# Down products with high and low parts as one moving operand of 512 columns

## The chip, the core and the metric

The kernel runs on one core of one Trainium2 chip. The metric is the device time of one execution in microseconds (us); a lower number is better. The engines named are TensorE (PE, matmuls), ScalarE (ACT), VectorE (DVE), GpSimd (POOL) and SyncE (SP, which issues the loads of weights).

## The reference

A first block of two layers, then a second block of two layers, on 256 tokens of width 1024 in float32. Only the feed-forward parts matter here. Block 1 has two per layer, one ahead of its mixer and one behind it:

```python
def swiglu(x, w1, w2):
    gu = x @ w1
    g, u = gu[..., :D_FF], gu[..., D_FF:]
    return (jax.nn.silu(g) * u) @ w2

for l in range(DEPTH):                       # DEPTH = 2, D_FF = 2816
    x = x + 0.5 * swiglu(rms_norm(x, ffn1_norm[l]), ffn1_w1[l], ffn1_w2[l])
    x = x + hybrid_mixer(rms_norm(x, mix_norm[l]), ...)
    x = x + 0.5 * swiglu(rms_norm(x, ffn2_norm[l]), ffn2_w1[l], ffn2_w2[l])
return rms_norm(x, final_norm)
```

Block 2 has one feed-forward part per layer, with a short convolution over the tokens between its two products, and a norm behind the second. The change leaves its products as they are.

## The kernel before, in words

**Data.** Everything is kept transposed: a tile is 128 features (partitions) x 256 tokens (T). x has 8 such tiles (KT), the hidden layer of a feed-forward part 22 (FT). To keep float32 accuracy on the faster fp32r matmul, each operand is split into a high part (rounded to fp32r) and a low part (what is left). A product (`product`, L600 to L607) of one 128x128 weight block with one tile is three matmuls of 256 columns into the same 256 columns of a bank: high weights x high part (L605), high weights x low part (L606), low weights x high part (L607). A bank (`banks`) holds 512 columns, used as two halves of 256.

**Weights.** They come as a stream of units of up to 16 blocks, 1 MB; the down units have 11 blocks, 704 KB. SP loads a unit into one of two raw slots (`load_unit`, L568), as soon as the unit two before it has been split. ACT casts it to `w_hi` (`split_hi`, L578) and DVE subtracts to get `w_lo` (`split_lo`, L584). There are four split slots; the cast of a unit waits until TensorE is done with the unit four before it. TensorE waits for `w_lo` (`weights_ready`). Every engine runs its own program in a fixed order written out by hand; semaphores alone tie them together. So on ACT and DVE the splits stand in a fixed place between the other work.

**A feed-forward part** (`ffn_pe`, `ffn_act`, `ffn_dve`). Up: 22 units, each 8 blocks for the gate half and 8 for the other half, into the halves of banks 0 to 3 in turn. DVE scales a bank by the norm (L835), ACT applies SiLU (L799), DVE multiplies the halves to `hid` (L840), ACT casts to `hid_hi` (L802), DVE subtracts to `hid_lo` (L846). Down: 8 output tiles, each 2 units of 11 blocks, so 22 products into columns 0 to 255 of bank 2 or 3 in turn. When a tile is done, DVE adds half the bank to x (`residual`, L865) and frees the bank; ACT squares the new x for the next norm (L721) and makes the next input's high part `h_hi` (L690), DVE its low part `h_lo` (L695). GpSimd sums the squares (L732).

**Order around the down products.** ACT: cast of the tile's first unit, square and h_hi of the tile, cast of its second unit. DVE: w_lo of the first unit, the residual, w_lo of the second, h_lo. The splits run four units ahead, so the last ones belong to what comes next: the mixer's `pa` units behind the first feed-forward part of a layer, the next layer's up units (or block 2's first units) behind the second. Behind the first part TensorE goes on with the mixer's products tile by tile (L640 to L642), and comes to the norm's matmuls after four tiles (48 matmuls). Behind the second part of layer 0 it starts the next up units (L617, L619), and these wait until banks 0 to 3 are all free.

**Loops.** TensorE's up loop is 2 units by `first_products` and then 5 rounds of 4 units; the down loop has 4 rounds of 2 tiles. ACT and DVE have 4 rounds of 4 units in the up part with the rest written out.

`Groups` and `Work` do the bookkeeping of which bank a group of products takes and who frees it; `wait_banks_free` and `bank_free` read it.

Of the kernel before, what the change touches and what calls it, by code (L numbers as in the profile page):

```python
# [23 lines left out]
T = 256  # L24
# [95 lines left out]
class Groups:  # L120


    def __init__(self, steps, freer=FREER, fixed=FIXED_BANK):
        self.mark, self.bank, self.freer = {}, {}, {}
        marks = 0
        self.freed_until, main, last, self.before = {"a": 0, "v": 0}, 0, {}, {}
        for kind, i in steps:
            g = (kind, i)
            if kind in NOT_ON_PE:
                continue  # L130
            if kind == "K":
# [22 lines left out]
            self.before[g] = last.get(bank)  # L154
# [4 lines left out]
            last[bank] = g  # L159
        self.marks, self.last = marks, last  # L160
# [119 lines left out]
def build(nc, io):  # L280
    with ExitStack() as ctx:
# [8 lines left out]
        h_hi = sbuf("h_hi", [P, KT, T], F32R)  # L290
        h_lo = sbuf("h_lo", [P, KT, T], F32R)
# [110 lines left out]
        class Work:  # L402
# [15 lines left out]
            def bank_free(self, layer, group):  # L418

                before = self.g.before[group]  # L420
                wrapped = before is None
                before = before or self.g.last[self.g.bank[group]]
                who, n = self.g.freer[before]
                s = self.freed[who]
                return s(layer, n - s.per) if wrapped else s(layer, n)

            def wait_banks_free(self, pe, layer, groups, taken=()):
# [6 lines left out]
                for group in groups:  # L434
                    before = self.g.before[group]
                    wrapped = before is None
                    who, n = self.g.freer[before or self.g.last[self.g.bank[group]]]
                    latest[who] = max(latest.get(who, -10 ** 9), n - (self.freed[who].per if wrapped else 0))
# [169 lines left out]

        def first_products(pe, nm, work, l, m, groups, stat):
# [131 lines left out]
        def ffn_pe(pe, work, nm, l, w, at, n, m, hidden, raw_units):  # L741
# [11 lines left out]

            work.wait_banks_free(pe, l, [(up, j) for j in range(4)])
            weights_ready(pe, at + 1)
            if raw_units:
# [7 lines left out]
                with pe.Fori(0, 4) as it:  # L764
                    for u in range(4):
                        pe.wait_ge(*work.taken(l, (up, 0), it * 4 + u))
                        up_unit(4 + u, it * 4)
                for j in range(20, FT):
                    pe.wait_ge(*work.taken(l, (up, j - 4)))
                    up_unit(j, 0)  # L770
            else:
                first_products(pe, nm, work, l, m, [((up, j), at + j) for j in range(2)], lambda: norm_pe(pe, work, nm, l, n))
                with pe.Fori(0, 5) as it:
                    for u in range(4):
                        pe.wait_ge(*work.taken(l, (up, 0), it * 4 + (2 + u - 4)))
                        up_unit(2 + u, it * 4)
            with pe.Fori(0, KT // 2) as it:
                for g in range(2):
# [3 lines left out]
                    for half in range(2):  # L782
# [3 lines left out]
                        for b in range(HALF):  # L786
                            k = half * HALF + b
                            if k >= FT - 3:
                                pe.wait_ge(*hidden(l, w * FT + k + 1))
                            last = product(pe, banks[2 + g][:, 0:T], s, b, hid_hi[:, k], hid_lo[:, k],  # L790
                                           k == 0, k == FT - 1)
                        last.then_inc(work.done_sem.sem, 1)

        def ffn_act(act, l, w, at, then, split):
# [8 lines left out]

            with act.Fori(0, 4) as it:
                for u in range(4):
                    gated(u, it * 4, u % 2, lambda: split_hi(act, at + u + FFN_AHEAD, it * 4, it * 2))
            split.next = at + 16 + FFN_AHEAD
            for j in range(16, FT):
# [20 lines left out]
        def ffn_dve(dve, l, w, at, n, then, split):  # L829
            up, down, work = f"up{w}", f"down{w}", work1  # L830

            def gated(j, more, parity, split_next, before=True):
                bank = banks[j % 4]
                dve.wait_ge(*work.done(l, (up, 0), more + j))
                dve.tensor_tensor(halves(scaled[:, parity]), halves(bank[:, :]), by_r(2),  # L835
# [14 lines left out]
            for j in range(2):  # L850
                gated(j, 0, j % 2, lambda: split.until(at + j + FFN_AHEAD), j > 0)
            with dve.Fori(0, 4) as it:
                for u in range(2, 6):
                    gated(u, it * 4, u % 2, lambda: split_lo(dve, at + u + FFN_AHEAD, it * 4))
            split.next = at + 18 + FFN_AHEAD
            for j in range(18, FT):
# [1466 lines left out]
```

## Time and profile before

| | us |
|---|---|
| median of 3 runs | 2327.35 |
| lowest and highest | 2321.9, 2327.54 |
| the profiled execution's own time | 2319.62 |
| its span, first to last instruction | 2317.8 |
| TensorE busy | 2045.6 (88%) |
| VectorE busy | 1472.7 (64%) |
| ScalarE busy | 1168.3 (50%) |
| mean granted TensorE clock | 0.931 |

Times of rows are us from the start of the span. Matmuls are pipelined: the duration of one (280 ns) is its way through the array, and what it costs in a stream is the distance between two starts. "Idle before" is idle time of the engine ahead of an instruction, with what ended it. The chain of waits is followed back from the last instruction, at each step to what released it. PEclk is the granted clock, 1.00 being 2.4 GHz and 0.50 being 1.2 GHz.

### The profile page before, as it was taken

Reading aid. Unit: us, or ns where it says so; the run is one execution under the profiler, and the core shown is the slowest. Engines: PE = TensorE matmul, PEld = TensorE weight load, DVE = VectorE, ACT = ScalarE, POOL = GpSimd, SP = SyncE. Lnnn points to the kernel's source line nnn. Section 1 sums busy time; section 2 is a strip of 40 time slices with the busy share of each in tenths; the row PEclk is TensorE's granted clock in tenths of the full one; section 3 lists DMA queues with packets and bytes.
Section 4 is the critical chain, followed back from the end, with each engine's and each line's share of the span. In section 5 each row is a group of like instructions: output and inputs, shape, how many; then the busy total and the mean of one; then the engine's idle time right before and its main releaser. Section 6 shows DMA issues by size and latency. Waiting matters only on the chain.

```text
span 2317.8 us, 40039 instructions
## 1 busy us (share of the span) xinstructions
PE 2045.6 (88%) x15496; PEld 1951.3 (84%) x15496; DVE 1472.7 (64%) x2084; ACT 1168.3 (50%) x1804; POOL 149.5 (6%) x167
## 2 busy tenths in 40 slices
PE   6999877879999999878879998787899978887998
PEld 6999867879999999867879998665799976667998
DVE  5665698655655655698656655564598465626963
ACT  5445644444444445644444445554565445536753
POOL 0071000000000001000000001000300000003000
PEclk9999989989999999989989999887899988878999
DMA  5545323345545545323345454331254532202543
GB/s 206 182 167 184 128 100 109 118 165 173 178 163 191 184 162 184 128 100 110 123 161 180 170 170 156 109 109 37 73 197 157 190 125 98 103 19 106 210 147 118
DMA packets 53535, 329.83 MB, mean 142 GB/s; under 512 B 5936, under 2 KB 6704, under 8 KB 27952
## 3 DMA queue, kind: packets, MB, share of 16 engines
q1 hardware_dynamic: 53424, 328.34, 41.0%
q8 instruction: 71, 1.16, 0.2%
q14 instruction: 40, 0.33, 0.0%
HBM read 327.27 MB, written 1.05 MB: 142 GB/s over the span
## 4 chain that ended last, share of the span: by engine, by line
PE 49%; DVE 16%; ACT 12%; issue 10%; DVEq 7%; DMA 3%; POOLq 3%; POOL 1%; ACTq 0%; SPq 0%
PE bank L605 13%; PE bank L606 13%; PE bank L607 13%; DVE w_lo L584 7%; ACT w_hi L578 5%; DMA raw<-in_w 2%; DVEq L915 2%; DVE conv L1239 2%; DVEq L1233 2%; PE bank L617 1%; ACT probs L924 1%; PE bank L626 1%; PE bank L619 1%; PE bank L1522 1%; PE bank L1538 1%
## 5 line engine op out<-in xcount | busy, mean ns | idle before, releaser
L584 DVE TENSOR_TENSOR w_lo<-raw,w_hi 128x2048 fp32r<-128x2048 f32 (+3 forms) x358 | 719.2, 2010 | 433.1 <-ACT w_hi L578 430.6
L605 PE MATMUL bank<-h_hi,w_hi 128*128 128x256 f32 x2704 | 784.9, 290 | 17.7 <-DVE w_lo L584 16.4
L606 PE MATMUL bank<-h_lo,w_hi 128*128 128x256 f32 x2704 | 775.7, 287 | 0.0
L607 PE MATMUL bank<-h_hi,w_lo 128*128 128x256 f32 x2704 | 774.9, 287 | 0.0
L578 ACT ACTIVATE w_hi<-raw 128x2048 fp32r<-128x2048 f32 (+3 forms) x358 | 600.9, 1680 | 170.7 <-DMA raw<-in_w 118.3
L605 PEld LDWEIGHTS bank<-h_hi,w_hi 128*128 128x128 f32 x2704 | 531.2, 196 | 23.2 <-DVE w_lo L584 17.5
L606 PEld LDWEIGHTS bank<-h_lo,w_hi 128*128 128x128 f32 x2704 | 531.0, 196 | 1.0
L607 PEld LDWEIGHTS bank<-h_hi,w_lo 128*128 128x128 f32 x2704 | 529.9, 196 | 0.0
L605 PE MATMUL bank<-hid_hi,w_hi 128*128 128x256 f32 x1056 | 296.2, 281 | 6.5 <-DVE conv L1879 6.5
L606 PE MATMUL bank<-hid_lo,w_hi 128*128 128x256 f32 x1056 | 296.2, 280 | 0.0
L607 PE MATMUL bank<-hid_hi,w_lo 128*128 128x256 f32 x1056 | 296.1, 280 | 0.0
L605 PEld LDWEIGHTS bank<-hid_hi,w_hi 128*128 128x128 f32 x1056 | 199.2, 189 | 6.9 <-issue 6.9
L607 PEld LDWEIGHTS bank<-hid_hi,w_lo 128*128 128x128 f32 x1056 | 199.3, 189 | 0.0
L606 PEld LDWEIGHTS bank<-hid_lo,w_hi 128*128 128x128 f32 x1056 | 199.2, 189 | 0.0
L799 ACT ACTIVATE scaled<-scaled 128x256 f32<-128x256 f32 x88 | 37.0, 420 | 263.5 <-DVE scaled L835 263.5
L922 ACT ACTIVATE probs<-probs,row 128x128 f32<-128x128 f32 x64 | 25.8, 404 | 189.2 <-DVE row L917 189.0
L728 POOL TENSOR_TENSOR acc<-sq 128x256 f32<-128x256 f32 x15 | 12.7, 847 | 1602.7 <-ACT sq L721 1602.5
L1239 DVE SCALAR_TENSOR_TENSOR conv<-glu,vec,conv 128x256 f32<-128x256 f32 x240 | 107.0, 481 | 10.5 <-issue 0.9
L721 ACT ACTIVATE sq<-x 128x256 f32<-128x256 f32 (+1 forms) x88 | 36.3, 412 | 136.7 <-DVE x L865 93.3
L835 DVE TENSOR_TENSOR scaled<-bank,rinv 128x512 f32<-128x512 f32 x88 | 60.6, 689 | 65.9 <-PE bank L607 41.2
L617 PE MATMUL bank<-h_hi,w_hi 128*128 128x256 f32 x192 | 56.1, 323 | 47.7 <-DVE w_lo L584 20.2
L617 PEld LDWEIGHTS bank<-h_hi,w_hi 128*128 128x128 f32 x192 | 43.8, 228 | 49.6 <-issue 32.0
(356 smaller groups left out, 3275.2 us busy)
## 6 DMA issues: line engine op xcount, KB each, us to landing
raw<-in_w SPq DMA_DIRECT2D x198, 1024.0 KB, 4.8
raw<-in_w SPq DMA_DIRECT2D x96, 704.0 KB, 4.0
raw<-in_w SPq DMA_DIRECT2D x52, 768.0 KB, 4.2
raw<-in_w SPq DMA_DIRECT2D x8, 512.0 KB, 3.5
raw<-in_w SPq DMA_DIRECT2D x4, 576.0 KB, 3.9
x<-in_x SPq DMA_DIRECT2D x1, 1024.0 KB, 4.7
out<-x SPq DMA_DIRECT2D x4, 256.0 KB, 2.4
const<-in_const SPq DMA_DIRECT2D x1, 548.0 KB, 5.2
```

The costliest lines, as they stand in the source:

```text
L578: act.activation(w_hi[:, s % SPLIT_SLOTS, 0:n], raw[:, s % RAW_SLOTS, 0:n], ACT.Copy).then_inc(stream.hi_ready.sem, 1)
L584: dve.tensor_tensor(w_lo[:, s % SPLIT_SLOTS, 0:n], raw[:, s % RAW_SLOTS, 0:n], w_hi[:, s % SPLIT_SLOTS, 0:n].bitcast(F32), ALU.subtract).t ...
L605: pe.matmul(out, hi, x_hi, start=start, stop=False)
L606: pe.matmul(out, hi, x_lo, start=False, stop=False)
L607: return pe.matmul(out, lo, x_hi, start=False, stop=stop)
L617: pe.matmul(out, w_hi[:, s % SPLIT_SLOTS, at], h_hi[:, k], start=k == 0 and half == 0, stop=False, skip_group_check=half == 1)
L721: act.activation(sq[:, parity], src, ACT.Square).then_inc(nm.sq_ready.sem, 1)
L799: act.activation(scaled[:, parity, 0:T], scaled[:, parity, 0:T], ACT.Silu).then_inc(silu_ready.sem, 1)
L835: dve.tensor_tensor(halves(scaled[:, parity]), halves(bank[:, :]), by_r(2), ALU.mult).then_inc(work.freed["v"].sem, 1)
L915: dve.drain()
L1233: dve.drain()
L1239: last = dve.scalar_tensor_tensor(conv[:, t], glu[:, t, j:j + T], w, conv[:, t], ALU.mult, ALU.add)
```

## The change

In block 1's down products, one matmul of 512 columns takes the place of L605 and L606: high weights x (high part, low part) side by side, into all 512 columns of the bank. The third matmul, low weights x high part, adds to columns 0 to 255. For that the high and the low part of a tile have to lie next to each other, so `hid_hi` and `hid_lo` become views of one tensor `hid_pair`, and `h_hi` and `h_lo` of `h_pair` (the h products stay as they are). The residual then adds both halves of the bank to x, one after the other, with a drain between. TensorE's up loop in block 1 has 4 rounds instead of 5 with units 2, 3, 20 and 21 written out; ACT and DVE write out units 0 to 3, 20 and 21. The bookkeeping of banks is written for groups that could take several banks; each still takes one.

```diff
-        h_hi = sbuf("h_hi", [P, KT, T], F32R)
-        h_lo = sbuf("h_lo", [P, KT, T], F32R)
+        h_pair = sbuf("h_pair", [P, KT, 2, T], F32R)
+        h_hi, h_lo = h_pair[:, :, 0], h_pair[:, :, 1]
...
-            hid_hi = sbuf("hid_hi", [P, FT, T], F32R, phase)
-            hid_lo = sbuf("hid_lo", [P, FT, T], F32R, phase)
+            hid_pair = sbuf("hid_pair", [P, FT, 2, T], F32R, phase)
+            hid_hi, hid_lo = hid_pair[:, :, 0], hid_pair[:, :, 1]
...
+        def pair_product(pe, bank, s, block, pair, start, stop):
+
+            hi = w_hi[:, s % SPLIT_SLOTS, block * P:block * P + P]
+            lo = w_lo[:, s % SPLIT_SLOTS, block * P:block * P + P]
+            pe.matmul(bank[:, 0:2 * T], hi, pair.rearrange("p a t -> p (a t)"), start=start, stop=False)
+            return pe.matmul(bank[:, 0:T], lo, pair[:, 0], start=False, stop=stop)
...
+            paired = work is work1
...
-                with pe.Fori(0, 5) as it:
-                    for u in range(4):
-                        pe.wait_ge(*work.taken(l, (up, 0), it * 4 + (2 + u - 4)))
-                        up_unit(2 + u, it * 4)
+                first = 2
+            for j in range(first, 4):
+                up_unit(j, 0)
+            with pe.Fori(0, 4) as it:
+                for u in range(4):
+                    pe.wait_ge(*work.taken(l, (up, 0), it * 4 + u))
+                    up_unit(4 + u, it * 4)
+            for j in range(20, FT):
+                pe.wait_ge(*work.taken(l, (up, j - 4)))
+                up_unit(j, 0)
...
-                            last = product(pe, banks[2 + g][:, 0:T], s, b, hid_hi[:, k], hid_lo[:, k],
-                                           k == 0, k == FT - 1)
+                            if paired:
+                                last = pair_product(pe, banks[2 + g], s, b, hid_pair[:, k], k == 0, k == FT - 1)
+                            else:
+                                last = product(pe, banks[2 + g][:, 0:T], s, b, hid_hi[:, k], hid_lo[:, k],
+                                               k == 0, k == FT - 1)
...
             def residual(t, more):
 
                 dve.wait_ge(*work.done(l, (down, 0), more * 2 + 2 * t))
+                dve.scalar_tensor_tensor(x[:, more + t], banks[2 + t % 2][:, T:2 * T], 0.5, x[:, more + t], ALU.mult, ALU.add)
+                dve.drain()
                 dve.scalar_tensor_tensor(x[:, more + t], banks[2 + t % 2][:, 0:T], 0.5, x[:, more + t], ALU.mult,
                                          ALU.add).then_inc(work.freed["v"].sem, 1)
```

## Rows read from the trace of the kernel before

**Rows 1.** The page: share of the span; matmuls by line; the DMA issues of down units.

```profile
PE 2045.6 (88%) x15496; PEld 1951.3 (84%) x15496; DVE 1472.7 (64%) x2084; ACT 1168.3 (50%) x1804; POOL 149.5 (6%) x167
...
L605 PE MATMUL bank<-h_hi,w_hi 128*128 128x256 f32 x2704 | 784.9, 290 | 17.7 <-DVE w_lo L584 16.4
...
L605 PE MATMUL bank<-hid_hi,w_hi 128*128 128x256 f32 x1056 | 296.2, 281 | 6.5 <-DVE conv L1879 6.5
...
raw<-in_w SPq DMA_DIRECT2D x96, 704.0 KB, 4.0
```

**Rows 2.** Windows: us, busy time and instructions by engine, PEclk, DMA share, GB/s.

```profile
540.00:651.00 111.00, 111.00 (x928) 111.00 (x927) 72.28 (x80) 48.99 (x60) 0.00 (x0) 1.00 0.51 177
...
651.57:713.40 61.83, 61.83 (x529) 61.83 (x528) 33.47 (x33) 29.23 (x32) 4.43 (x6) 1.00 0.57 192
...
716.90:720.30 3.40, 3.40 (x19) 3.40 (x17) 1.92 (x2) 3.21 (x3) 0.00 (x0) 0.51 0.88 311
```

**Rows 3.** Timeline, TensorE, stage 2: start, duration, line, tiles, idle before and releaser.

```profile
651.57 0.28 PE L605 MATMUL bank<-hid_hi,w_hi 128*128 128x256 f32 x1
...
713.41 0.28 PE L607 MATMUL bank<-hid_hi,w_lo 128*128 128x256 f32 x1
...
716.23 0.39 PE L617 MATMUL bank<-h_hi,w_hi 128*128 128x256 f32 x1 [2.54 <-DVE x L865]
```

**Rows 4.** Chain of waits, end of stage 2: start, duration, what.

```profile
694.36 1.40 ACT w_hi L578
...
706.80 4.77 DMA raw<-in_w
...
713.55 2.29 DVE w_lo L584
...
715.84 0.34 DVE x L865
```

**Rows 5.** Timeline, VectorE in stages 2, 3 and 1, TensorE where stages 3 and 1 end.

```profile
694.91 0.48 DVE L695 SCALAR_TENSOR_TENSOR h_lo<-x,const,h_hi  x1
...
695.78 1.63 DVE L584 TENSOR_TENSOR w_lo<-raw,w_hi 128x1408 fp32r<-128x1408 f32 x1 [0.39 <-ACT w_hi L578]
...
904.15 2.29 DVE L584 TENSOR_TENSOR w_lo<-raw,w_hi 128x2048 fp32r<-128x2048 f32 x1 [1.08 <-ACT w_hi L578]
...
909.99 0.42 DVE L865 SCALAR_TENSOR_TENSOR x<-bank,x 128x256 f32<-128x256 f32 x1
...
907.34 0.28 PE L640 MATMUL bank<-h_hi,w_hi 128*128 128x256 f32 x1
...
208.07 2.29 DVE L584 TENSOR_TENSOR w_lo<-raw,w_hi 128x2048 fp32r<-128x2048 f32 x1 [1.07 <-ACT w_hi L578]
...
211.48 0.28 PE L640 MATMUL bank<-h_hi,w_hi 128*128 128x256 f32 x1
```

**Rows 6.** Timeline, TensorE: 512-column products of block 2, then 256-column h products.

```profile
1468.30 0.39 PE L654 MATMUL bank<-w_hi,h_hi 128*128 128x512 f32 x1
...
1468.98 0.39 PE L654 MATMUL bank<-w_hi,h_hi 128*128 128x512 f32 x1
...
600.09 0.28 PE L605 MATMUL bank<-h_hi,w_hi 128*128 128x256 f32 x1
...
600.21 0.28 PE L606 MATMUL bank<-h_lo,w_hi 128*128 128x256 f32 x1
```

**Rows 7.** Timeline, VectorE in block 2: two instructions before a drain and one behind it.

```profile
1763.34 0.47 DVE L1879 SCALAR_TENSOR_TENSOR conv<-bank,vec,conv 128x255 f32<-128x255 f32 x1
1763.98 0.48 DVE L1879 SCALAR_TENSOR_TENSOR scaled<-bank,vec,scaled 128x254 f32<-128x254 f32 x1 [0.17 <-issue]
```

**Rows 8.** Timeline, ScalarE in stage 1, VectorE and ScalarE in stage 4.

```profile
192.94 1.38 ACT L578 ACTIVATE w_hi<-raw 128x1408 fp32r<-128x1408 f32 x1 [1.46 <-DMA raw<-in_w]
...
1381.23 1.63 DVE L584 TENSOR_TENSOR w_lo<-raw,w_hi 128x1408 fp32r<-128x1408 f32 x1 [0.60 <-ACT w_hi L578]
...
1387.32 1.39 ACT L578 ACTIVATE w_hi<-raw 128x1408 fp32r<-128x1408 f32 x1 [1.02 <-PE bank L607]
```

More of the change, by code:

```diff
@@ L153, in __init__ @@
             self.mark[g], self.bank[g] = marks, bank
-            self.before[g] = last.get(bank)
+            taken = (bank,)
+            self.before[g] = [(b, last.get(b)) for b in taken]
             if who is None:
@@ L158, in __init__ @@
             self.freer[g] = (who, self.freed_until[who])
-            last[bank] = g
+            for b in taken:
+                last[b] = g
         self.marks, self.last = marks, last
@@ L418, in bank_free @@
             def bank_free(self, layer, group):
-                before = self.g.before[group]
+                (bank, before), = self.g.before[group]
                 wrapped = before is None
-                before = before or self.g.last[self.g.bank[group]]
-                who, n = self.g.freer[before]
+                who, n = self.g.freer[before or self.g.last[bank]]
                 s = self.freed[who]
@@ L433, in wait_banks_free @@
                     latest[who] = max(latest.get(who, n), n)
-                for group in groups:
-                    before = self.g.before[group]
+                for bank, before in (b for group in groups for b in self.g.before[group]):
                     wrapped = before is None
-                    who, n = self.g.freer[before or self.g.last[self.g.bank[group]]]
+                    who, n = self.g.freer[before or self.g.last[bank]]
                     latest[who] = max(latest.get(who, -10 ** 9), n - (self.freed[who].per if wrapped else 0))
@@ L763, in ffn_pe @@
                 by_tiles(pe, work, l, [((up, 3), at + 3)], lambda k: nm.true_ready(l, k + 1))
-                with pe.Fori(0, 4) as it:
-                    for u in range(4):
[L766 to L770, printed above, removed]
+                first = 4
             else:
                 first_products(pe, nm, work, l, m, [((up, j), at + j) for j in range(2)], lambda: norm_pe(pe, work, nm, l, n))
-                with pe.Fori(0, 5) as it:
-                    for u in range(4):
-                        pe.wait_ge(*work.taken(l, (up, 0), it * 4 + (2 + u - 4)))
-                        up_unit(2 + u, it * 4)
+                first = 2
[8 more added lines that the diff above has]
+                up_unit(j, 0)
             with pe.Fori(0, KT // 2) as it:
@@ L802, in gated @@
                 act.activation(hid_hi[:, more + j], hid[:, parity], ACT.Copy).then_inc(hid_hi_ready.sem, 1)
+            for j in range(4):
+                gated(j, 0, j % 2, lambda: split.until(at + j + FFN_AHEAD))
             with act.Fori(0, 4) as it:
-                for u in range(4):
+                for u in range(4, 8):
                     gated(u, it * 4, u % 2, lambda: split_hi(act, at + u + FFN_AHEAD, it * 4, it * 2))
-            split.next = at + 16 + FFN_AHEAD
-            for j in range(16, FT):
+            split.next = at + 20 + FFN_AHEAD
+            for j in range(20, FT):
                 gated(j, 0, j % 2, lambda: split.until(at + j + FFN_AHEAD))
@@ L849, in ffn_dve @@
             dve.wait_ge(*n1.std_ready(l, n + 1))
-            for j in range(2):
+            for j in range(4):
                 gated(j, 0, j % 2, lambda: split.until(at + j + FFN_AHEAD), j > 0)
             with dve.Fori(0, 4) as it:
-                for u in range(2, 6):
+                for u in range(4, 8):
                     gated(u, it * 4, u % 2, lambda: split_lo(dve, at + u + FFN_AHEAD, it * 4))
-            split.next = at + 18 + FFN_AHEAD
-            for j in range(18, FT):
+            split.next = at + 20 + FFN_AHEAD
+            for j in range(20, FT):
                 gated(j, 0, j % 2, lambda: split.until(at + j + FFN_AHEAD))
```

3 lines of the change are left out of this document (1 added, 2 removed).

## The prediction, made before the changed kernel was run

> **What bounds the kernel now.** I read the page first: TensorE is busy 88% of the span [rows 1], so I asked where it is bound and where it waits. The change touches four stretches, the down products of block 1's four feed-forward parts; I call them stages 1 to 4. A stage is 8 output tiles x 2 weight units x 11 blocks x 3 matmuls = 528 matmuls. The windows view shows stage 2 as solid TensorE work at full clock [rows 2], and the timeline gives its pitch: the first matmul starts at 651.57, the last at 713.41 [rows 3], so 61.84 us for 527 steps, 117.3 ns each. At 2.4 GHz 256 columns take 106.7 ns; 10.7 ns per matmul are extra. The other three stages repeat this, with the same length to 0.1 us.
>
> The chain of waits then says what sets each stage's end, and it is not TensorE. In stage 2 the chain leaves TensorE at 694.36, where ACT's cast of the stage's 15th weight unit has waited for TensorE to finish the 11th; from there it runs w_lo, DMA (4.8 us), cast, w_lo, DMA, cast, w_lo, and only then the last residual and the next stage's first matmul at 716.23 [rows 3, 4]. TensorE idles 2.8 us before it. So of 61.8 us only those before the 11th unit's end pay in stage 2; the last 20 us of TensorE work lie beside the weight stream (two raw slots, each refilled once w_lo is made). Stage 4 ends the same way. After stages 1 and 3 TensorE goes on without a gap into the mixer (907.34, 211.48), whose weights (18th unit) were ready at 904.15 + 2.29 = 906.44 and 208.07 + 2.29 = 210.36: only 0.9 and 1.1 us before [rows 5].
>
> **The change, part by part.**
>
> *One matmul fewer per product.* Per product three matmuls of 256 columns, 3 x 117.3 = 352.0 ns, become one of 512 and one of 256. Block 2 already streams 512 columns of such data: from 1468.30 to 1468.98 three of them take 680 ns, 226.7 ns each [rows 6]. I take 226.7 + 117.3 = 344.0, a saving of 8.0 ns (2.3% of the stage). Upper bound: the 512-column one keeps the 10.7 ns extra of these rows' own matmuls: 224.0 + 117.3, saving 10.7. Lower bound: both come at the 13.3 ns extra that the h products show (120.0 ns from 600.09 to 600.21 [rows 6]): 346.7, saving 5.3. Per stage (176 products) TensorE gets 1.41 us shorter (0.93 to 1.88), and its 11th unit (121 products) ends 0.97 us sooner (0.64 to 1.29). Dropped weight loads are not counted again: they overlap the matmuls, and the pitch has them in it.
>
> The Trainium skill ("TensorE: Matmul & The Clock Gate", section "Back-to-back issue gap") gives the gap as columns/2.4 plus about 2.5 ns. By that the pair would save only 2.5 ns a product, 1.8 us of TensorE in all; the trace disagrees with its 10.7 ns at 256 columns, and the sum goes by the trace; by the page's 2.5 ns it would come to +0.2 us.
>
> *The residual becomes two adds with a drain between.* One add from a bank is 0.42 us (909.99 [rows 5]); in block 2 the same kind of instruction follows another after a drain 0.64 us later start to start (1763.34 to 1763.98) where its own length is 0.47 [rows 7]. So 0.42 + 0.17 = 0.59 us more for each of 32 residuals. Between 0.42 (drain free) and 0.64. TensorE does not wait for it inside a stage: the two banks alternate and a bank has 7.6 us. DVE has room (34 of 62 us busy [rows 2]), but what is queued behind a residual moves: ACT's square, h_hi and the next odd cast, then DVE's odd w_lo and the h_lo behind it. The even w_lo, which carries the chain, starts at 695.78 right after that h_lo (694.91 + 0.48) [rows 5]. New: residual 4 starts 0.88 earlier (110 products) and is 0.59 longer, so h_lo ends at 695.39 - 0.88 + 0.59 = 695.10, while the cast would be done at 694.81. So w_lo gains 0.66 instead of 0.97.
>
> *Ends of the stages.* Stage 2: chain 0.66 sooner, last residual 0.59 longer, next matmul waits for that residual's bank: -0.1 us. Stage 3: TensorE would arrive at 907.34 - 1.41 = 905.93; the 18th unit's cast stands behind residual 6 on ACT, so its w_lo ends at 906.44 - 0.66 + 0.59 = 906.37; start about 906.42: -0.9. Later waits there hold: the norm comes 48 matmuls on, 5.8 us, at 912.2, the last residual (909.99 now [rows 5]) ends about 910.3, its square 0.5 later. Stage 1: the casts at its end wait for their DMA, not for TensorE (192.94 [rows 8]), so they don't follow TensorE; nothing there gains, residual 6 is 0.59 longer: weights at 210.95, start at 211.0 instead of 211.48: -0.5. Stage 4: the 13th unit's w_lo starts only at 1381.23, and with 1.63 of its own, 0.17 to issue, 4.0 of DMA and 0.1 to start the 15th can be cast at 1387.1, against 1387.32 now [rows 8]; gain 0.1 to 0.2, minus 0.59: +0.4, or -0.1 if the transfers run as in stage 2. I take +0.2.
>
> *Loops and layout.* TensorE's up loop goes from 5 rounds to 4 with four units written out; the window over that loop has 928 matmuls in 111.0 us [rows 2], 120 ns, with its edges in it, so nothing. ACT and DVE keep four rounds; only which are written out moves. h_pair and hid_pair take the same bytes as the two tensors each replaces, in another order; 0.
>
> **Sum:** -0.5 - 0.1 - 0.9 + 0.2 = -1.3 us. With the bounds of the saving: 5.3 ns gives -0.5, +0.2, -0.65, +0.35 = -0.6; 10.7 ns gives -0.5, -0.4, -1.2, 0 = -2.1. The profiled execution took 2319.62 us (span 2317.8 and 1.8 around it), so 2318.3 on its scale. The median shown is 2327.35, 7.7 above it, so the forecast is 2327.35 - 1.3 = 2326.0.
>
> One cost I can't fix is the clock. After the 2.8 us idle in stage 2 the granted clock is 0.51 from 716.9 to 720.3 [rows 2], 1.2 instead of 2.4 GHz, which costs half of 3.4 us, 1.7 us. The idle grows to 4.2 us (TensorE ends 1.4 sooner, starts as before), stage 4's as much. One such stretch more or fewer is +-1.7.
>
> **Rivals.**
> A. TensorE sets all four ends: the weight stream speeds up with it and the second add hides. Then 4 x 1.41 to 1.88 = -5.6 to -7.5, 2320 to 2322. For: TensorE never waits inside a stage. Against: the chain above, which leaves it 20 us before the end. 0.12.
> B. Slower: the weight stream becomes the bound. One slot's round is DMA 4.0, cast 1.39, w_lo 1.63, about 0.3 of issue and semaphores: 7.3 us [rows 1, 4, 5] against TensorE's 7.73 per two units now and 7.57 after. It decides where a round is over 7.57, as when a transfer takes 0.3 us longer. Then stages 2 and 4 gain nothing and pay 0.59, stage 3 starts at 907.08 (-0.3), stage 1 -0.5: +0.4, and with TensorE idling up to 4.8 us in stage 2 and more in stage 4 one or two more half-clock stretches: +2.1 to +3.8, 2329.4 to 2331.2. 0.14.
> C. The extra 10.7 against 13.3 ns comes from where operands lie, and the new order of h and hid changes it. If the 8112 h matmuls (2704 x 3 [rows 1]) went from 120.0 to 117.3: -21.6, less what their stages hide, 2306. If hid went to 120.0: block 2's two stages pay 1056 x 2.7 = +2.8, block 1 as at the 5.3 ns bound, -0.6: 2329.6. Against: within each the extra is the same for all tiles, and tile addresses keep their 1 KB steps. 0.04 and 0.03.
> D. It doesn't save: 512 columns of hid cost two passes of 256. Then stages 2 and 4 pay 0.59 each: +1.2, 2328.5. Against: the 512-column rows. 0.05.
>
> **How the numbers follow.** The forecast has 0.62. A measurement of this kernel can tell about 0.3%, 7 us, from no change; the three runs span 5.6. Faster by more needs C's first half, the far end of A, or luck in the runs: 0.10. Slower by more needs B with something added: 0.06. Same: 0.84. The range 2319 to 2331 takes in A, B, D and the clock; the forecast's own is 2323.5 to 2328.5.
>
> **What would show it.** Right: in a stage, starts 227 then 117 ns apart, 704 fewer matmuls and loads, a stage of 60.4 us; residual pairs 0.59 apart; idle before the next feed-forward near 4.2 us in stage 2, and a new short idle (0.5 to 0.9 us) at the mixers' start waiting on w_lo. Wrong: a stage under 60 or over 61 us; h products off 120.0 ns; casts inside stages 2 and 3 that wait for DMA instead of TensorE (B); a mixer start 1.4 us sooner (A).

## The result: slower, by 0.28%

The changed kernel took a median of 2331.43 us (2323.94 to 2338.78, 17 runs) against 2325.94 us (2321.25 to 2331.19, 17 runs) of the kernel before on the same chip. The ratio is 1.0028, with an interval of 1.0014 to 1.0041: some 6.5 us slower. I had forecast 1.3 us faster.

The profiled execution of the changed kernel took 2329.74 us, with a span of 2327.9. That is 10.1 us over the span of the profile before; the two profiles are single executions, and the one before had been 6 us below its own median. Executions of one program lie up to 17 us apart, and the longer ones have in most cases the lower mean granted clock (the six shortest of the changed kernel 0.925 to 0.933, the six longest 0.921 to 0.925), so differences of a few us rest on medians of 8 to 33 executions, never on two. What I read from them is therefore what recurs in the experiments further down, not the 10.1 as such.

The page of the changed kernel: the busy line, three matmul groups and the loads of down units (columns as in [rows 1]).

```profile
PE 2049.5 (88%) x14792; PEld 1926.8 (83%) x14792; DVE 1490.8 (64%) x2116; ACT 1170.8 (50%) x1804; POOL 151.2 (6%) x167
...
L605 PE MATMUL bank<-h_pair,w_hi 128*128 128x256 f32 x2704 | 786.3, 291 | 16.8 <-DVE w_lo L584 16.7
...
L613 PE MATMUL bank<-hid_pair,w_hi 128*128 128x512 f32 x704 | 244.3, 392 | 0.0
L614 PE MATMUL bank<-hid_pair,w_lo 128*128 128x256 f32 x704 | 196.8, 280 | 0.0
...
raw<-in_w SPq DMA_DIRECT2D x96, 704.0 KB, 4.0
```

The change does what it says: 704 matmuls fewer, and 704 of the rest have 512 columns. Yet TensorE's busy time is up by 3.9 us instead of down by 3.7 (704 x 5.3 ns, measured below). Busy time counts a matmul at half clock as longer, so I went from the page to the timeline, TensorE in stage 2 (start, duration, line, tiles):

```profile
669.99 0.39 PE L613 MATMUL bank<-hid_pair,w_hi 128*128 128x512 f32 x1
670.22 0.28 PE L614 MATMUL bank<-hid_pair,w_lo 128*128 128x256 f32 x1
670.34 0.39 PE L613 MATMUL bank<-hid_pair,w_hi 128*128 128x512 f32 x1
...
718.06 0.28 PE L614 MATMUL bank<-hid_pair,w_lo 128*128 128x256 f32 x1
724.12 0.58 PE L624 MATMUL bank<-h_pair,w_hi 128*128 128x256 f32 x1 [5.78 <-DVE x L879]
```

A product takes 0.35 us (670.34 - 669.99); averaged over the 704 pairs, 229.3 + 117.4 = 346.7 ns. The stage runs without an idle moment from 657.15 to 718.06, 60.91 us, 0.93 less than in [rows 3]. Then TensorE idles 6.06 us, against 2.82 (716.23 - 713.41 in [rows 3]). The same arithmetic for all four stages, each time from its first matmul (an idle of 0.12 is the ordinary distance of two matmuls, so no idle):

| | first to last matmul, before and after | idle behind it, before and after | start to next part, change |
|---|---|---|---|
| stage 1 | 61.84, 60.91 | 0.12, 3.85 | +2.80 |
| stage 2 | 61.84, 60.91 | 2.82, 6.06 | +2.31 |
| stage 3 | 61.84, 60.91 | 0.12, 1.49 | +0.44 |
| stage 4 | 61.84, 60.91 | last residual ends at 65.26, 66.92 | +1.66 |

Three of these sum to +5.55. Of the rest of the 10.1 us, +1.01 lies ahead of stage 1 (this lead runs from 149.2 to 150.6 over all kernels that follow, with either product), and +1.77, +0.79 and +1.77 between the stages; from stage 4's start to the end the profile after is 0.79 shorter, its +1.66 included, so block 2 hid or made good that much. The first two leads between stages show the clock. Windows of the changed kernel behind stages 1 and 2 (columns as in [rows 2]):

```profile
215.29:219.29 4.00, 4.00 (x19) 4.00 (x20) 3.05 (x3) 0.81 (x2) 0.00 (x0) 0.50 0.73 250
...
724.12:728.12 4.00, 4.00 (x18) 4.00 (x19) 1.72 (x2) 3.95 (x4) 0.00 (x0) 0.50 0.79 266
```

and the same four microseconds of the kernel before:

```profile
211.48:215.48 4.00, 4.00 (x36) 4.00 (x35) 2.73 (x3) 1.31 (x4) 0.00 (x0) 1.00 0.76 268
...
716.23:720.30 4.07, 4.07 (x22) 4.07 (x22) 1.92 (x2) 3.88 (x4) 0.00 (x0) 0.59 0.74 260
```

Behind stage 1 TensorE was granted 2.4 GHz before and 1.2 GHz after, having now idled 3.85 us ahead of it: 19 matmuls in 4 us instead of 36. The stretch lasts until 220.7, so 5.4 us of work ran at half clock; at full clock they would have taken 2.7, and +1.77 is left of the difference at the end of the lead. Behind stage 2 a half-clock stretch was there already, 3.4 us of work (716.9 to 720.3), and is 5.2 us now (to 729.3). For the third (+1.77 behind stage 3) the granted clock is 1.00 in the first 20 us behind the idle. Part of it is the weight stream again: at 941.06, 24.6 us into that lead, TensorE waits another 0.47 us for w_lo, where the kernel before has no wait. Over all kernels of this study that lead is 436.7 to 437.3 us in the five below that have the odd cast ahead of the residual and 437.2 in the kernel before, and 438.2 to 439.9 in all the others.

So the question is why the weights came late. The chain of waits of the changed kernel at the end of stage 2 (start, duration, what), to be held against [rows 4]:

```profile
700.52 0.48 DVE h_pair L702
701.00 1.59 DVE w_lo L584
...
702.75 6.92 DMA raw<-in_w
709.67 0.02 issue
709.69 1.93 ACT w_hi L578
711.62 0.02 issue
711.64 2.30 DVE w_lo L584
...
714.11 4.86 DMA raw<-in_w
...
719.00 1.92 ACT w_hi L578
...
720.94 2.29 DVE w_lo L584
723.23 0.33 DVEq L878
723.56 0.07 issue
723.63 0.44 DVE x L879
```

The links at the end are the ones of before, but the first 1 MB load of the next part takes 6.92 us where it took 4.78. SP's queue in the changed kernel shows what goes ahead of it (issue, time, line):

```profile
700.79 0.33 SPq L568 DMA_DIRECT2D raw<-in_w  x1
...
702.75 0.33 SPq L568 DMA_DIRECT2D raw<-in_w  x1
```

and in the kernel before:

```profile
695.18 0.33 SPq L568 DMA_DIRECT2D raw<-in_w  x1
...
697.58 0.33 SPq L568 DMA_DIRECT2D raw<-in_w  x1
```

An output tile's second unit has an odd number, its first an even one. An odd unit's load goes out when the odd unit two before it is split, and the even one's right behind, when the even slot is free: 2.40 us apart before, 1.96 after. Stage 1 has the same at its end, less far (2.68 us apart before, 2.33 after; the 1 MB load took 6.03 us against 4.77), and inside the stages the even 704 KB loads took 5.14 to 5.51 us wherever they follow 1.9 to 2.1 us behind the odd one. From each start, stage 2's ledger is exact: this load is issued 0.41 sooner (45.60 for 46.01), takes 2.14 longer, the next one 0.09 longer, and the pair of adds ends 0.49 later: +2.31.

Why they moved together shows in the chain's first two lines. w_lo of the odd unit ends, and its slot's next load goes out; DVE makes the short h_lo, then w_lo of the even unit, and the second load goes out. Before, this second w_lo still waited for its cast, and that for TensorE ([rows 4, 5]). Now the odd cast comes later, since on ACT it stands behind the square and h_hi of a tile whose residual is two adds, and the even cast may come sooner, since TensorE is ahead. DVE then runs h_lo and w_lo back to back, and 1.9 to 2.0 us is all they take.

Stage 1 has a second cause. There are two buffers for squares, so ACT's square of a tile waits until GpSimd has summed the square two tiles before, and early in stage 1 GpSimd still has other work ahead of that sum. ScalarE in the kernel before, in the changed kernel and in e3_layout_only below (timeline):

```profile
174.85 0.42 ACT L721 ACTIVATE sq<-x 128x256 f32 x1 [3.47 <-POOL acc L728]
...
177.61 0.42 ACT L728 ACTIVATE sq<-x 128x256 f32 x1 [5.25 <-POOL acc L735]
...
176.12 0.42 ACT L728 ACTIVATE sq<-x 128x256 f32 x1 [5.78 <-POOL acc L735]
```

The odd cast stands behind that square. From the stage's start the square comes at 25.32, 27.07 and 26.88 us, and the odd load that hangs on it 1.74 us later in the changed kernel and 1.56 later in e3_layout_only than before. So most of what delays stage 1 up to its last loads is not the distance of two loads, and it is there without the 512-column product and without the second add.

### The profile page after: what moved, and what is told of

Its sections match the earlier page's. It is cut to its first block, busy times and chain, and to the rows that moved or that the text cites. A ratio compares the mean times of both kernels' runs of the same rounds, so it can differ in the third digit from the quotient of the medians.

```text
span 2327.9 us, 38759 instructions
## 1 busy us (share of the span) xinstructions
PE 2049.5 (88%) x14792; PEld 1926.8 (83%) x14792; DVE 1490.8 (64%) x2116; ACT 1170.8 (50%) x1804; POOL 151.2 (6%) x167
## 4 chain that ended last, share of the span: by engine, by line
PE 54%; DVE 17%; ACT 12%; DVEq 7%; issue 5%; DMA 4%; POOLq 1%; POOL 1%; ACTq 0%; SPq 0%
PE bank L605 13%; PE bank L606 13%; PE bank L607 13%; DVE w_lo L584 7%; ACT w_hi L578 5%; PE bank L613 4%; DMA raw<-in_w 4%; DVEq L929 2%; DVE conv L1253 2%; DVEq L1247 2%; PE bank L614 2%; PE bank L624 1%; PE bank L626 1%; PE bank L633 1%; ACT probs L938 1%
## 5 line engine op out<-in xcount | busy, mean ns | idle before, releaser
L605 PE MATMUL bank<-h_pair,w_hi 128*128 128x256 f32 x2704 | 786.3, 291 | 16.8 <-DVE w_lo L584 16.7
L606 PE MATMUL bank<-h_pair,w_hi 128*128 128x256 f32 x2704 | 777.6, 288 | 0.0
L607 PE MATMUL bank<-h_pair,w_lo 128*128 128x256 f32 x2704 | 776.5, 287 | 0.0
L605 PEld LDWEIGHTS bank<-h_pair,w_hi 128*128 128x128 f32 x2704 | 532.8, 197 | 22.4 <-DVE w_lo L584 18.0
L606 PEld LDWEIGHTS bank<-h_pair,w_hi 128*128 128x128 f32 x2704 | 532.5, 197 | 0.8
L607 PEld LDWEIGHTS bank<-h_pair,w_lo 128*128 128x128 f32 x2704 | 531.7, 197 | 0.0
L613 PE MATMUL bank<-hid_pair,w_hi 128*128 128x512 f32 x704 | 244.3, 392 | 0.0
L614 PE MATMUL bank<-hid_pair,w_lo 128*128 128x256 f32 x704 | 196.8, 280 | 0.0
L613 PEld LDWEIGHTS bank<-hid_pair,w_hi 128*128 128x128 f32 x704 | 132.1, 188 | 29.0
L614 PEld LDWEIGHTS bank<-hid_pair,w_lo 128*128 128x128 f32 x704 | 132.2, 188 | 0.0
L605 PE MATMUL bank<-hid_pair,w_hi 128*128 128x256 f32 x352 | 99.7, 283 | 6.5 <-DVE conv L1893 6.5
L624 PE MATMUL bank<-h_pair,w_hi 128*128 128x256 f32 x192 | 58.6, 333 | 51.1 <-DVE w_lo L584 20.3
L606 PE MATMUL bank<-hid_pair,w_hi 128*128 128x256 f32 x352 | 99.6, 283 | 0.0
L607 PE MATMUL bank<-hid_pair,w_lo 128*128 128x256 f32 x352 | 99.6, 283 | 0.0
```

Source lines behind the costliest of these rows:

```text
L605: pe.matmul(out, hi, x_hi, start=start, stop=False)
L606: pe.matmul(out, hi, x_lo, start=False, stop=False)
L607: return pe.matmul(out, lo, x_hi, start=False, stop=stop)
L613: pe.matmul(bank[:, 0:2 * T], hi, pair.rearrange("p a t -> p (a t)"), start=start, stop=False)
L614: return pe.matmul(bank[:, 0:T], lo, pair[:, 0], start=False, stop=stop)
L624: pe.matmul(out, w_hi[:, s % SPLIT_SLOTS, at], h_hi[:, k], start=k == 0 and half == 0, stop=False, skip_group_check=half == 1)
```

## The experiments

Theory P (pairing in time): the two loads are issued closer together and the second one then takes longer; the residual's extra add and TensorE's lead both push that way. Rivals: R (the second add and its drain cost by themselves, on DVE and at the end), L (the layout, the loops and the bookkeeping cost), and M (the 512-column matmul gives nothing or takes from elsewhere). The expectations call P "theory 1" or the collision. In the order of the runs; every ratio is to the kernel before, timed beside it.

| | median us | before | ratio | 95% interval | idle behind stages 1, 2, 3 |
|---|---|---|---|---|---|
| changed kernel | 2331.43 | 2325.94 | 1.0028 | 1.0014 to 1.0041 | 3.85, 6.06, 1.49 |
| e1_before_two_adds | 2333.38 | 2327.05 | 1.0043 | 1.0023 to 1.0064 | 0.32, 6.40, 0.11 |
| e2_after_one_add | 2329.71 | 2327.05 | 1.0014 | 0.9997 to 1.0030 | 4.05, 4.63, 0.12 |
| e3_layout_only | 2326.67 | 2327.05 | 1.0006 | 0.9990 to 1.0021 | 0.58, 3.00, 0.12 |
| e4_after_reordered | 2318.01 | 2327.05 | 0.9973 | 0.9956 to 0.9990 | 0.12, 1.30, 0.12 |
| e5_even_held | 2334.49 | 2327.09 | 1.0026 | 1.0008 to 1.0044 | 3.71, 4.66, 1.86 |
| e6_cast_first | 2323.08 | 2327.09 | 0.9991 | 0.9977 to 1.0005 | 0.12, 3.43, 0.12 |
| e7_last_residual_first | 2324.82 | 2327.09 | 1.0003 | 0.9983 to 1.0022 | 3.34, 1.76, 1.37 |
| e8_before_reordered | 2316.63 | 2327.09 | 0.9953 | 0.9938 to 0.9968 | 0.12, 0.79, 0.12 |
| e9_before_odd_held | 2331.83 | 2327.53 | 1.0021 | 1.0008 to 1.0034 | 1.19, 3.57, 0.32 |
| e10_even_held | 2331.29 | 2327.53 | 1.0020 | 1.0003 to 1.0038 | 2.27, 5.99, 0.39 |
| e11_after_reordered | 2320.88 | 2327.53 | 0.9973 | 0.9954 to 0.9991 | 0.12, 1.30, 0.12 |
| e12_before_reordered | 2315.56 | 2327.53 | 0.9953 | 0.9934 to 0.9972 | 0.12, 0.79, 0.12 |

**One part at a time.** The kernel before with a first add that adds nothing (factor 0.0) and the drain:

```diff
 dve.wait_ge(*work.done(l, (down, 0), more * 2 + 2 * t))
+dve.scalar_tensor_tensor(x[:, more + t], banks[2 + t % 2][:, 0:T], 0.0, x[:, more + t], ALU.mult, ALU.add)
+dve.drain()
```

> The kernel before, with a second add (of 0.0 x the same half bank) and a drain ahead of each residual: the vector cost of the change alone, products and layout untouched. Theory 1 (the longer residual holds up the odd casts, so that each even load is issued only about 2.0 us behind the odd one instead of 2.3 to 2.4, the two collide, and the weights of the stages' ends come late): slower than before by 3 to 9 us, 704 KB even loads at 5.0 to 5.5 us in part and the first 1 MB load of each stage's end at 6 to 7 us, TensorE idle about 5 us after stage 2. Theory 2 (the 512-column products and the new layout cost the time): within 1.5 us of before, loads of 4.0 and 4.8 us, idle 3.4 us after stage 2.

The changed kernel without its first add and the drain (the product of high weights and low part is then made, but not added):

```diff
-dve.scalar_tensor_tensor(x[:, more + t], banks[2 + t % 2][:, T:2 * T], 0.5, x[:, more + t], ALU.mult, ALU.add)
-dve.drain()
```

> The changed kernel without the first add and the drain, so the high-weights x low-part term of block 1's down products is left out of x. Theory 1: faster than before by 1 to 4 us, since the casts go as before and TensorE is 0.9 us a stage shorter; the even loads stay at 2.2 us or more behind the odd ones and at 4.0 and 4.8 us. Theory 2: as slow as the changed kernel, 4 to 8 us over before. Theory 3 (shorter TensorE stages alone bring the even loads too close to the odd ones): between, 2 to 4 us over before, with some loads over 5 us.

The changed kernel with three matmuls and one add, so that only layout, loops and bookkeeping are left of the change:

```diff
-            paired = work is work1
+            paired = False
...
-dve.scalar_tensor_tensor(x[:, more + t], banks[2 + t % 2][:, T:2 * T], 0.5, x[:, more + t], ALU.mult, ALU.add)
-dve.drain()
```

> The changed kernel's layout (h_pair, hid_pair) and loops with the old three products and one add. Theory 1: within 1.5 us of before; block 2's hid products 118.7 ns apart instead of 117.3 as in the changed kernel (1056 x 1.4 = 1.5 us), and block 1's too. Theory 2: 3 to 6 us over before.

A caution for all that follows: the leads ahead of block 2's two down stages vary from 381.9 to 395.2 us over the fourteen profiled executions, with no edit there, so I compare medians for the time and block 1's stages for the cause, never two spans.

Measured: the second add alone makes the kernel slower by 0.43%, the 512-column product alone by 0.14% with an interval that touches no change, the layout by 0.06%, none that can be told. So L is no large part, but it is not excluded: its interval reaches 0.21%, and its profile has the wait for GpSimd in stage 1 (idle 0.58 there). The add is the larger part (its median is 6.3 us above the kernel before), while the 32 adds, at 0.50 us, lie beside TensorE's work in all but the last tile of a stage. R by itself would give 0.5 us in each of the stages that the last residual ends; stage 2 of this profile is 3.58 us longer. The end of stage 2 in e1_before_two_adds, chain of waits:

```profile
698.72 7.54 DMA raw<-in_w
...
706.29 1.93 ACT w_hi L578
...
708.24 2.30 DVE w_lo L584
...
710.71 4.82 DMA raw<-in_w
```

This load was issued 2.19 us behind the one before it (696.53) and took 7.54 us: the long load is there without any 512-column matmul. In e2_after_one_add, with one add, 704 KB loads of 5.2 to 5.4 us and 1 MB loads of 5.5 to 6.8 are there as well. P covers these less well: but for one of them (1.92) they were issued 2.35 to 2.62 us behind the load ahead, where loads of the kernel before at 2.38 to 2.40 took 3.8 to 4.2 us for 704 KB, but for one of 5.03, and 4.78 for 1 MB. Both halves of the change come with long loads; that the product brings them by the distance alone isn't shown.

**Moving the loads apart.** On ACT, the cast of the odd unit goes ahead of the residual's square and h_hi, for tiles 0 to 6; on DVE, the last tile's residual goes ahead of the w_lo that stood before it:

```diff
 # ffn_act
                     split_hi(act, base + 2 * g, it * 4, it * 2)
-                    residual(g, it * 2)
                     split_hi(act, base + 2 * g + 1, it * 4, it * 2)
+                    residual(g, it * 2)
...
-                split.until(base + 2 * t)
+                split.until(base + 2 * t + (t == 6))
                 residual(t, 0)
 # ffn_dve
-                split.until(base + 2 * t)
+                if t < 7:
+                    split.until(base + 2 * t)
                 residual(t, 0)
+                split.until(base + 2 * t)
```

> The changed kernel with another order around its down products: on ScalarE the cast of a tile's second unit goes ahead of the square and h_hi of tiles 0 to 6; on VectorE the last tile's residual goes ahead of the w_lo before it. Theory 1: the odd casts no longer wait for the residual, so the even load is issued 3 us or more behind the odd one, no load of 704 KB takes over 4.4 us, TensorE idles under 1.5 us after stage 2: 6 to 12 us faster than the changed kernel, 1 to 6 us faster than before. Theory 2: within 2 us of the changed kernel.

Then each half alone, and both on the kernel before:

> The changed kernel with the scalar half of the reordering alone: the odd cast ahead of square and h_hi for tiles 0 to 6. Theory 1: loads over 3 us apart and at 4.0 to 4.3 us, first 1 MB load 4.8; TensorE idle after stage 2 at 3.5 to 4.2 us, since the last residual still stands behind a w_lo; 4 to 8 us faster than the changed kernel. Rival (the late last residual is what costs): under 2 us faster than the changed kernel.

> The changed kernel with the vector half of the reordering alone: the last tile's residual ahead of the w_lo before it. The loads collide as in the changed kernel (first 1 MB load 6 to 7 us), but at the ends of stages 2 and 4 the residual no longer waits for them: TensorE idle after stage 2 about 1.3 us instead of 6. Expected 4 to 8 us faster than the changed kernel if the ends of stages 2 and 4 carry most of the loss, under 3 if stages 1 and 3 do.

> The kernel before with both halves of the reordering: does the 512-column operand bring anything once the order is right? Theory 1: TensorE then sets most of the stages' ends; this is 4 to 8 us faster than before, and the changed kernel with the same order (0.9973 of before) is 0 to 4 us faster than this one (4 x 0.93 us of TensorE less, 0.5 us more in each last residual). If it is as fast or faster than that, the 512-column operand brings nothing even so.

Measured: with both halves, the changed kernel goes from 0.28% slower to 0.27% faster than the kernel before. In the profile the loads inside the stages are 2.8 us and more apart and the 704 KB ones take 3.7 to 4.4 us (one issued just ahead of stage 3 takes 5.68; see below). The ACT half alone takes the long loads away (the first 1 MB ones are at 4.7 to 4.9) and the idle behind stages 1 and 3 with them (in stage 1 it also takes the cast from behind the wait for GpSimd, and no run parts the two); behind stage 2 3.43 us stay, since the last residual still stands behind a 2.29 us w_lo. The DVE half alone takes that (1.76), while the 704 KB loads 1.9 us apart stay at 5.3 to 5.6 us. Each half removes the idle that it should and only that.

But the kernel before gains more from the same edit: 0.47%. So the long loads were no property of the 512-column product; the kernel before had some too (5.83 us at the end of stage 4, where its two loads are 2.25 apart), and it had the last residual behind w_lo. Its gain is 10.5 us by the medians. The profiles have 2.0 of it in stages 1 to 3, 1.5 in the lead behind stage 2, whose half-clock stretch is gone (127.7 for 129.2 us), and 2.7 at stage 4's last residual, if block 2 keeps them; where the rest comes from isn't shown. The repetition side by side:

> The changed kernel with both halves of the reordering, timed beside the next one on the same chip. TensorE then sets the ends of stages 1 and 3 and nearly that of 2, so its 0.93 us less a stage should show, against 0.5 us more in each last residual: 1 to 3 us faster than the next one if the operand is worth anything; within 1 us or slower if not.

> The kernel before with the same reordering, three products of 256 columns and one add: 8 to 13 us faster than before, as its first timing (0.9953) says. See the kernel beside it for the comparison.

2320.88 against 2315.56; 0.9973 and 0.9953 again, to the digit. The intervals overlap, but two pairs of runs say the same: with the better order the 512-column product is no gain, and probably a loss of 0.2%. The end of stage 2 in e12_before_reordered, TensorE and VectorE (timeline):

```profile
713.31 0.28 PE L607 MATMUL bank<-hid_hi,w_lo 128*128 128x256 f32 x1
714.10 0.39 PE L617 MATMUL bank<-h_hi,w_hi 128*128 128x256 f32 x1 [0.52 <-DVE x L865]
```

```profile
713.62 0.42 DVE L865 SCALAR_TENSOR_TENSOR x<-bank,x 128x256 f32<-128x256 f32 x1 [1.95 <-PE bank L607]
```

and TensorE in e4_after_reordered:

```profile
714.49 0.39 PE L624 MATMUL bank<-h_pair,w_hi 128*128 128x256 f32 x1 [1.01 <-DVE x L879]
```

Here the last matmul sets the end, and the idle is the residual alone: 0.79 with one add, 1.30 with two. From its start to the next part a stage 2 takes 62.63 us in the one and 62.20 in the other, stages 1 and 3 61.95 and 61.03. By the stages the pair should win 2.3 us up to stage 3; the two medians have it 1.4 and 5.3 us behind. Part of that is ahead of stage 2, where the profiles show 440.7 and 441.9 us for the pair and 439.4 and 439.6 without. It isn't the product: e3_layout_only, with three 256-column matmuls, has 441.0 there, and the five profiles with the old layout and loops have 439.4 to 440.5, against 440.3 to 443.2 with the new ones. Whether it's the layout or the loops, and where the rest of the difference comes from, stays open.

**The distance of the loads alone.** To move the loads and nothing else I held SP ahead of an issue. Waits that are already met, twelve of them, ahead of the even load:

```diff
+            if s in HELD:
+                for _ in range(12):
+                    sp.wait_ge(x_in.sem, 16)
```

> The changed kernel, where SyncE puts twelve waits that are already met (about 0.5 us) ahead of each even load of block 1's down units and of the first load behind them. If the collision of loads is the cost, a later issue pays: no 704 KB load over 4.5 us, first 1 MB loads of 4.8 to 5.5 us instead of 6.0 to 7.1, and the kernel 1 to 5 us faster than the changed one, although each load starts 0.5 us later. If the loads are slow for another reason, or the late casts alone cost the time, it is 1 to 4 us slower than the changed kernel.

This was a miss. In the trace they are six instructions, 0.06 us apart, that SP ran at 702.55 to 702.89, ahead of the one that waits for w_lo (704.37): the even load still went out 0.17 us behind w_lo, and in each stage at least one went out 1.9 to 2.0 us behind the odd one. It is a repetition of the changed kernel, and as such it agrees in time (1.0026); its idle of 4.66 behind stage 2, for 6.06, shows how far two profiles of the same order can differ. Increments of an unused semaphore do hold SP, 0.06 us each. First on the kernel before, ahead of each odd load, to bring the two closer together:

```diff
+            if s in HELD:
+                for _ in range(6):
+                    sp.sem_inc(held_sem.sem, 1)
             sp.dma_start(raw[:, s % RAW_SLOTS, 0:n], src).then_inc(stream.raw_full[s % RAW_SLOTS].sem, 16)
```

> The kernel before, with six increments of an unused semaphore (0.3 to 0.6 us) on SyncE ahead of each odd load of block 1's down units; nothing else. This brings the even load closer behind the odd one with no change on TensorE, VectorE or ScalarE. If the collision is the mechanism: even loads 1.8 to 2.1 us behind the odd ones take 5.0 to 5.6 us (704 KB) and 6 to 7 us (first 1 MB), TensorE idles 4 to 6.5 us after stage 2, 3 to 10 us slower than before. If closeness doesn't matter: within 2 us of before, loads of 4.0 and 4.8 us.

and on the changed kernel, the same lines ahead of each even load, to bring them apart:

> The changed kernel with the same six increments ahead of each even load of the down units and of the first load behind them. Collision theory: the loads are 2.3 us or more apart, no 704 KB load over 4.5 us, the first 1 MB load 4.8 to 5.5 us, and 1 to 6 us faster than the changed kernel although every round of the even slot is 0.3 to 0.6 us longer. Otherwise 1 to 4 us slower than it.

Measured for e9_before_odd_held: slower by 0.21% with no edit on TensorE, ACT or DVE. SP's queue early in stage 2, and the second load in the chain of waits:

```profile
665.81 0.33 SPq L574 DMA_DIRECT2D raw<-in_w  x1
...
667.83 0.33 SPq L574 DMA_DIRECT2D raw<-in_w  x1
```

```profile
667.83 5.05 DMA raw<-in_w
...
673.00 1.39 ACT w_hi L584
```

The odd loads issued later are not on the chain; the even ones, issued when they were before, take 5.05 to 5.70 us where they are 1.8 to 2.2 us behind the odd ones, and the 1 MB ones 6.35 and 7.48. The chain of stage 2 now goes through every even load from this one on, where before it left TensorE only at 694.36 [rows 4]. A load that is closer behind another is enough to make the kernel slower: that is P by itself. It is smaller than P had it: 3.57 us of idle behind stage 2, where I expected 4 to 6.5, and stages 1 to 3 are 2.0 us longer in the profile, of 4.3 between the medians.

For e10_even_held P had the loads back at 4 us, and nearly they are: no 704 KB load above 4.94 us, no 1 MB load behind one above 5.09. The median is no lower for it, though (2331.29, where P had 1 to 6 us less than the changed kernel). The end of stage 2, chain of waits:

```profile
694.28 4.10 DMA raw<-in_w
698.48 1.39 ACT w_hi L584
...
699.89 1.63 DVE w_lo L590
...
702.07 4.78 DMA raw<-in_w
```

From one even load to the next is 7.79 us (702.07 - 694.28): 4.10 of transfer, 1.39 and 1.63 of splitting, 0.55 from w_lo to the issue (0.17 without the hold, so the hold is 0.38), and the semaphores. TensorE needs 7.63 for the two units (22 x 0.3467). In stage 2 holding the load costs as much as it saves: the first 1 MB load is issued 1.75 us later than in the changed kernel (47.35 for 45.60 from the stage's start) and takes 2.14 less. Stages 1 and 3 do come out 1.6 and 1.1 us shorter in this profile, which is one of the shortest of its twelve executions (2323.66); the medians don't show it.

The distances and durations of every load behind a 704 KB one, from the traces of all fourteen profiled executions (least, median, greatest):

| issued behind the one before, us | 704 KB | 1 MB |
|---|---|---|
| 1.8 to 2.0 | 4.35, 5.35, 5.70 (20) | 6.64, 7.01, 7.48 (6) |
| 2.0 to 2.2 | 4.54, 5.14, 5.45 (8) | 6.35, 6.78, 7.54 (4) |
| 2.2 to 2.4 | 3.84, 4.22, 5.39 (35) | 4.83, 5.68, 6.51 (15) |
| 2.4 to 2.6 | 3.80, 4.06, 4.92 (30) | 4.78, 4.83, 4.87 (3) |
| 2.6 to 2.8 | 3.85, 4.11, 4.46 (43) | 4.71, 4.80, 6.78 (6) |

Farther apart the medians stay at 4.0 to 4.1 and 4.8 to 4.9. Away from the down products it is the same: five 1 MB loads in every one of the fourteen are issued 2.0 to 2.4 us behind another 1 MB load and take 5.73 us in the median (70 loads), against 4.80 at 4 to 6 us (1615 loads). That the second load is slowed by the first is read from these numbers and from e9_before_odd_held, where the distance was set by hand. What in the transfer makes it so was not tried.

Single loads farther apart are slow as well, and they have another companion. DMA view of the changed kernel during a 704 KB load that was issued 4.56 us behind the one before it (852.76 to 858.1; queue and kind, packets, MB, share of 16 engines; then the issue):

```profile
q1 hardware_dynamic: 144, 0.72, 38.0%
q8 instruction: 1, 0.02, 1.8%
...
raw<-in_w SPq DMA_DIRECT2D x1, 704.0 KB, 5.3
```

A small transfer of the kind "instruction" falls into it. Of the 3849 loads of 704 KB or 1 MB that the fourteen traces have 2.6 us or more behind the one before, 150 take over 4.7 or over 5.2 us; 135 of the 150 have such a transfer in flight, and 774 of all. Of the 38 loads in the table's first two rows only 3 have one, so it isn't what slows the close pairs.

## Why the prediction was wrong

*One matmul fewer per product.* The size was at my lower bound: 346.7 ns a product, 5.3 saved, not 8.0; 0.93 us a stage instead of 1.41. The 512-column matmul comes at 229.3 ns, not at block 2's 226.7 [rows 6]. This alone would have moved the sum from -1.3 to -0.6.

*The residual.* Two adds start 0.48 to 0.52 us apart (714.34 after 713.85), so +0.50, inside my bounds of 0.42 to 0.64 and under my 0.59. The mechanism that I named, that what is queued behind the residual moves, is the right one; I followed it for the even w_lo and did not ask what it does to the distance between the two loads.

*Ends of the stages.* This is the step that failed. I took 4.0 us (704 KB) and 4.77 us (1 MB) as fixed prices of a transfer, whenever it is issued. In stage 2 I had the even w_lo 0.66 sooner and the residual 0.59 longer, -0.1. The issue did come sooner, 0.41, and the residual was 0.49 longer, but the load took 2.14 us longer and the next one 0.09: +2.31. Stage 1: -0.5 forecast, +2.80 measured: the 1 MB load was issued 2.06 later, took 1.26 longer, the residual added 0.50, and 1.02 of the 3.82 went into slack that the weights had had. Of the 2.06, 1.74 are there already when the odd cast comes late behind ScalarE's wait for GpSimd, a wait that the prediction hadn't looked for (3.47 us in the kernel before) and put at nothing. Stage 3: -0.9 forecast, +0.44, with a load of 6.75 us where 5.59 stood. Stage 4: +0.2 forecast, +1.66, with a load of 7.10 us where 5.83 stood. All four have the same sign; in stages 2, 3 and 4 the longer load is the cause, in stage 1 it is one of two. The page of the profile could not have shown it: it says 4.0 us for the 704 KB loads before and after, a median over 96 of them.

*The clock.* I had +-1.7 for one half-clock stretch more or less, and there is one more, behind stage 1, where I had forecast no idle to speak of; its lead is 1.77 longer. The stretch behind stage 2 is the old one with 1.8 us more of work in it.

*Loops and layout.* Nothing that the time shows, as forecast (e3_layout_only: 1.0006, with an interval up to 1.0021), though the wait in stage 1 and a lead of 441.0 ahead of stage 2, for 440.1, came with them. The h products stay at 120 ns, so rival C has no part in it.

*Rivals.* A would need the stream to speed up with TensorE; it got slower. D is out: two passes of 256 columns would be 234.6 ns, and the matmul comes at 229.3. B is nearest to what happened, by its own condition: a transfer 0.3 us longer decides. I priced it at +0.4 to +3.8 and gave it 0.14, because I let the transfer cross the threshold and did not ask how far it would go. The medians have +5.5 and the ratio about +6.5. The kernel before held the warning: in its chain, the first 1 MB loads at the ends of stages 3 and 4 take 5.59 and 5.83 us, those of stages 1 and 2 4.77 and 4.78. I took that for scatter. The slow two were issued 2.26 and 2.25 us behind the load ahead, the other two 2.68 and 2.40.

## What to carry to other kernels

A transfer's duration belongs to its place in the queue: before a ring of two buffers is called slack enough, list the distance of each issue to the one before it beside its duration, and ask what the edit does to that distance. An engine that gets ahead, or work that is put between two splits, can push two loads together, and then the ring's round grows by more than the edit saved. Where one engine makes both the weights' split and the chain's last step, the order of the two is worth more (0.47% here, from moved lines alone) than a matmul saved on an engine that isn't the one to wait for; the best version of this study is the kernel before in that order, 2316.63 and 2315.56 us.

## What the runs showed of the hardware

- Two loads from one queue 1.8 to 2.2 us apart: the second takes 5.0 to 5.7 us for 704 KB (23 of 28) instead of 4.0, and 6.4 to 7.5 us for 1 MB (10 of 10) instead of 4.8. From 2.2 to 2.4 both kinds occur; from 2.4 us on the medians are back at 4.1 and 4.8, and so they stay, with single loads up to 5.7 and 6.8.
- Most slow loads that are not close behind another (135 of 150) have a small transfer of the queue's kind "instruction" in flight with them.
- In the pair, a 512-column fp32r matmul costs 229.3 ns and the 256-column one behind it 117.4.
- Behind an idle of 3.85 us the granted clock was 0.50, 1.2 GHz, for the next 5.4 us (x19 matmuls in the first 4 us instead of x36); behind 1.49 us it stayed at 1.00, 2.4 GHz.
- Waits on SP that were already met and stood behind the open wait for w_lo in the program ran ahead of it in the trace (702.55 to 702.89, before 704.37) and held nothing; a semaphore increment takes 0.06 us there (0.38 for six).
